# A hybrid decoder trunk on one core: the second layer's state chain in two stretches of four chunks in place of four of two

## What is computed

```python
r, k, v, z = rkvz[0], rkvz[1], rkvz[2], rkvz[3]      # xm[p] @ w[p], four projections
logw = -jax.nn.softplus(-(w0 + jnp.tanh(xm[4] @ w1) @ w2)) - 0.5
a = jax.nn.sigmoid(a0 + (xm[5] @ a1) @ a2)
...
def step(state, inp):
    rt, wt, kt, vt, kkt, at = inp
    sa = jnp.einsum("bhvk,bhk->bhv", state, -kkt)
    state = (state * wt[:, :, None, :] + sa[..., None] * (kkt * at)[:, :, None, :]
             + vt[..., None] * kt[:, :, None, :])
    return state, jnp.einsum("bhvk,bhk->bhv", state, rt)
...
out = (y * jax.nn.silu(z)) @ rw_w_out[j]
```

## Time and profile before

| what | value |
|---|---|
| median of three runs | 3538.35 us (3529.3 to 3553.95) |
| the profiled execution | 3545.52 us |
| its span in the profile | 3543.7 us |
| mean granted clock of TensorE | 0.971 |
| TensorE, matmuls | 3286.5 us busy, 93% |
| VectorE | 1604.9 us busy, 45% |
| ScalarE | 1314.0 us busy, 37% |
| GpSimd | 222.4 us busy, 6% |

### The profile page before, as it was taken

The page is one execution under the profiler, slowest core; times in us unless marked ns, Lnnn a source line. Parts: engine busy times, 40 slices in busy tenths (PEclk is TensorE's granted clock), DMA queues, the critical chain, the costliest instruction groups (busy, mean ns, idle before and its releaser), DMA issues.

```text
span 3543.7 us, 80467 instructions
## 1 busy us (share of the span) xinstructions
PE 3286.5 (93%) x35338; PEld 1989.4 (56%) x35338; DVE 1604.9 (45%) x3443; ACT 1314.0 (37%) x2492; POOL 222.4 (6%) x345
## 2 busy tenths in 40 slices
PE   2899999999999968999999999999999999999998
PEld 1555465556455535666566466556466656556663
DVE  7245254435534544344564244554244454244442
ACT  0343344343434353333453133444133453223332
POOL 0010001010001000000000000000000000000000
PEclk8999999999999988999999999999999989999999
DMA  8231322331224131112112212112212112121111
GB/s 333 73 97 49 120 84 85 96 97 48 82 86 121 49 108 38 39 39 63 38 39 68 79 39 63 26 51 63 78 39 67 33 39 62 46 77 39 39 61 42
DMA packets 275862, 247.53 MB, mean 70 GB/s; under 512 B 16253, under 2 KB 251961, under 8 KB 272953
## 3 DMA queue, kind: packets, MB, share of 16 engines
q1 hardware_dynamic: 273208, 233.99, 21.0%
q0 software_dynamic: 2304, 8.39, 0.7%
HBM read 217.17 MB, written 25.18 MB: 68 GB/s over the span
## 4 chain that ended last, share of the span: by engine, by line
PE 75%; DVE 12%; DMA 5%; ACT 5%; issue 2%; SPq 1%; DVEq 0%; ACTq 0%; another core or an unknown queue 0%
PE bank L679 20%; PE bank L539 14%; PE bank L648 7%; PE bank L765 4%; PE bank L778 4%; PE bank L536 3%; PE bank L774 3%; DVE xm L1561 3%; PE bank L568 2%; DVE arena L1622 2%; PE bank L690 2%; DMA xm<-in_ada_w 2%; PE bank L820 1%; DMA arena<-residual_scratch 1%; DVE arena L1632 1%
## 5 line engine op out<-in xcount | busy, mean ns | idle before, releaser
L679 PE MATMUL bank<-xm,wring 128*128 128x512 f32 x2048 | 933.6, 604 | 0.8 <-ACT arena L1104 0.8
L679 PEld LDWEIGHTS bank<-xm,wring 128*128 128x128 f32 x2048 | 383.2, 192 | 474.8 <-issue 462.4
L539 PE MATMUL bank<-arena,wring 128*128 128x512 f32 x1280 | 580.0, 593 | 12.5 <-ACT xm L969 5.1
L539 PEld LDWEIGHTS bank<-arena,wring 128*128 128x128 f32 x1280 | 231.0, 190 | 256.7 <-issue 246.0
L648 PE MATMUL bank<-wring,yT 128*128 128x512 f32 x776 | 340.2, 599 | 16.7 <-DVE yT L1681 5.4
L648 PEld LDWEIGHTS bank<-wring,yT 128*128 128x128 f32 x776 | 148.1, 192 | 204.9 <-issue 188.6
L1150 ACT COPY arena<-bank 128x256 f32<-128x256 f32 x256 | 96.4, 377 | 440.3 <-PE bank L778 440.3
L1837 POOL COPY r_Q<-ident 128x512 f32<-128x512 f32 x160 | 98.1, 613 | 2017.4 <-PE bank L778 2015.5
L1662 DVE COPY arena<-bank 128x64 f32<-128x64 f32 x256 | 57.3, 224 | 348.6 <-PE bank L810 342.8
L778 PE MATMUL bank<-arena,r_Q 64*64 64x32 f32 x5120 | 201.8, 222 | 0.2 <-issue 0.2
L765 PE MATMUL bank<-arena 64*64 64x32 f32 x5120 | 191.4, 221 | 1.6 <-DVE arena L1646 1.1
(11 more groups left out here) (278 smaller groups left out, 5097.2 us busy)
## 6 DMA issues: line engine op xcount, KB each, us to landing
wring<-in_rw_w_rkvz SPq DMA_DIRECT2D x128, 512.0 KB, 3.9
wring<-in_ev_w_in SPq DMA_DIRECT2D x96, 512.0 KB, 5.2
xm<-in_ada_w SPq DMA_DIRECT2D x16, 1536.0 KB, 12.0
wring<-in_ev_w_out SPq DMA_DIRECT2D x32, 512.0 KB, 5.3
wring<-in_rw_w_out SPq DMA_DIRECT2D x32, 512.0 KB, 5.5
layer_input<-arena SPq DMA_DIRECT2D x4, 2052.0 KB, 7.7
wring<-layer_input SPq DMA_DIRECT2D x16, 513.0 KB, 7.2
xm<-in_x POOLq DMA_DIRECT2D x16, 512.0 KB, 5.3
```

Source lines behind the costliest of these rows:

```text
L539: mm = pe.matmul(pj[:, :], w[:, k, :], hT[:, k, 1:1 + TB], start=(k == 0), stop=(k == KC - 1))
L679: mm = pe.matmul(bank[1 if m == PROJ_Z else 0][:, :], w[:, k, :], xmv[MIX_OF[m]][:, k, :], start=(k == 0), stop=(k == KC - 1))
```

## The change

Three lists of work change their order, one for each engine, and no instruction is added or removed. On TensorE quarter 0 comes behind projection K and the second gate matmul instead of in front of them, and quarter 2 comes behind projection Z instead of in front of it. The chunks of a unit then run as 0 to 3 and 4 to 7, with the key sum and projections R and Z in one run between them. ScalarE and VectorE have their parts moved likewise: gate, K's copy, the squares and both sigmoids in front of quarter 0; R's copy, decays, rates, finish and bonus in front of quarter 2. `INV_CUT`, the waits within the helpers, and SyncE's and GpSimd's programs stay as they are.

```diff
--- before.py
+++ after.py
@@ -876,20 +876,20 @@
                 if not inv:
                     pe.wait_ge(S["b0_free"], turn(BANK0, "v", v) + 1)
                     pe.wait_ge(S["b1_free"], turn(BANK1, "var", v - 1) + 1)
-                quarter(v, 0)
                 if pre:
                     lora_up(v + 2, 0)
                     project(v + 2, PROJ_K, 0, KC)
                     lora_up(v + 2, 1)
+                quarter(v, 0)
                 quarter(v, 1)
                 if pre:
                     key_sum(v + 2)
                     project(v + 2, PROJ_R, 0, KC)
-                quarter(v, 2)
                 if inv:
                     project(v + 1, PROJ_Z, 0, KC)
                 else:
                     pe.wait_ge(S["r_done"], 1 + v)
+                quarter(v, 2)
                 quarter(v, 3)
                 if (v + 3) % RP == 0 and v + 3 < NU:
                     lora_down((v + 3) // RP)
@@ -1186,7 +1186,6 @@
                     act.copy(r_yd, bank[1][:, :]).then_inc(S["b1_free"], 1)
                 if inv:
                     project_evac(v + 1, PROJ_V)
-                quarter_act(v, 0)
                 if pre:
                     lora_evac(v + 2, 0)
                 if v >= 0:
@@ -1199,6 +1198,7 @@
                     project_evac(v + 2, PROJ_K)
                     key_squares(v + 2)
                     lora_evac(v + 2, 1)
+                quarter_act(v, 0)
                 quarter_act(v, 1)
                 if pre:
                     act.wait_ge(S["r_tbm"], v + 3)
@@ -1213,7 +1213,6 @@
                     mix(B, MIX_W, 0, 5)
                 if second_:
                     mix(B, MIX_V, 0, 5)
-                quarter_act(v, 2)
                 if pre:
                     project_evac(v + 2, PROJ_R)
                     decays(v + 2)
@@ -1224,6 +1223,7 @@
                     mix(B, MIX_A)
                 if second_:
                     mix(B, MIX_V, 5, KC)
+                quarter_act(v, 2)
                 quarter_act(v, 3)
                 if inv:
                     project_evac(v + 1, PROJ_Z)
@@ -1701,7 +1701,6 @@
                     mix(B, MIX_K, 3, KC)
                 if inv:
                     rwkv_masks(v + 1)
-                rwkv_quarter(v, 0)
                 if v >= 0:
                     rwkv_gate(v)
                 if pre:
@@ -1710,6 +1709,7 @@
                     mix(B, MIX_R)
                 if third:
                     mix((v + 1) // RP, MIX_Z)
+                rwkv_quarter(v, 0)
                 rwkv_quarter(v, 1)
                 if pre:
                     rwkv_key(v + 2)
@@ -1717,7 +1717,6 @@
                     mix(B, MIX_W, 0, 5)
                 if second_:
                     mix(B, MIX_V, 0, 5)
-                rwkv_quarter(v, 2)
                 if pre:
                     rwkv_rates(v + 2)
                 if v >= 1:
@@ -1729,6 +1728,7 @@
                     mix(B, MIX_A)
                 if second_:
                     mix(B, MIX_V, 5, KC)
+                rwkv_quarter(v, 2)
                 rwkv_quarter(v, 3)
                 own.restart()
```

## The result

The changed kernel takes 3567.9 us, the median of 15 runs (3550.7 to 3580.8). The kernel before took 3553.95 in the 15 runs beside it (3529.3 to 3557.6). The ratio is 1.0052, with a 95% interval of 1.0035 to 1.0069 (the two medians lie 0.4% apart): slower by half a per cent, where the forecast, 3535 for 3538.35, was a ratio of 0.999. The profiled span went from 3543.7 to 3566.1 us and the mean granted clock from 0.971 to 0.961.

What follows compares the result with a forecast made beforehand. TensorE, busy for 93% of the span, was taken as the bound. Terms -0.8 (plain), +3, -2, 0, -1, +1 and -4 (clock) sum to -3.8 us: 3535 us from 3538.35; own range 3522 to 3550, stated range 3510 to 3575.

Steps and rivals of the forecast that it cites:

- Step 1: Plain period, chunk 0: the key run in front covers the masks' tail, gate and scan, so TensorE's wait goes, -0.49 us.
- Step 3: Plain period, chunk 1 to chunk 2: the joint loses its cover and line 810 waits for the new state, +0.34 us.
- step 4: Plain period, chunk 5 to chunk 6: line 810 likewise waits for VectorE's new state, +0.31 us.
- step 5: Plain period, R and Z joined in one run: one change of tile size in and one out are gone, -0.20 us.
- Steps 2, 6 and 7: Plain period: V's copy before K, other engines' work beside R and Z, and weight loads all stay hidden, no cost.
- v = 5, 13 and 21: Eleven mixes now before quarter 2: wait about 6.9 us against 5.3 and some 0.6; +1.0 each, +3 in all.
- v = 15: Periods with Z mixes: their wait of a microsecond moves from chunk 2 to chunk 0, net 0.
- The clock, -4: Of three half-clock falls behind chunk 0's idle time (v = 14, 22, 23), one was expected to go, -4 us.
- v = 14: Key run covers chunk 0's losses, but R's mixes leave 1.3 us idle there: net -0.7, three times, -2 us.
- Unit 30: Without K, 1.5 us of sigmoid idle time moves from chunk 2 to chunk 0; chunk 4 gets Z in front: -1 us.
- The falling clock: Rival, chance 0.14: clock falls in longer small-tile stretches, once per plain period +90 us, 3625 us; in both stretches 3715.
- The joints' rival: Rival, chance 0.12: exposed joints cost more, 1.3 us a plain period in all, giving 3561 us.

Runs made afterwards that it cites:

- e3: New order in the 21 plain periods only, old order in the others, against the kernel before: 3543.1 us, ratio 0.9976.
- e2: Only the second move (quarter 2 behind projection Z), quarter 0 left where it was, against the kernel before: 3566.7 us, ratio 1.0045.
- e7: Kernel before with idle VectorE additions put in front of chunk 2 in 13 plain periods: 3611.9 us, one run.
- e4: New order only in periods 5 to 7, 13 to 15, 21 to 23, 30 and 31, against the kernel before: 3575.4 us, ratio 1.0072.
- e1: Only the first move (quarter 0 behind the key run), quarter 2 left where it was, against the kernel before: 3545.4 us, ratio 0.9977.
- e13: Changed kernel, mixes whole, with an inverse part moved into the last gap of chunks 1 and 5: 3535.5 us, ratio 0.9946 to the kernel before.
- e6: Changed kernel with idle VectorE additions put in front of chunk 0 in 13 plain periods: 3678.3 us, one run.
- e8: Changed kernel with R and Z mixes split in halves and an inverse part in both joints' gaps: 3510.9 us, ratio 0.9899 to the kernel before.
- e10: First move only, R and Z mixes split, one inverse part in the last gap of chunk 1, against the kernel before: 3506.5 us, ratio 0.9883.
- e11: First move, split mixes and filled gap of chunk 1, but old order in v = 30 and 31, against the kernel before: 3503.9 us, ratio 0.987.

## Why the prediction was wrong

**The plain period** was right in kind and nearly so in size. Step 1 said -0.49 for chunk 0; it measured -0.75 (2.77 for 3.52 from line 810 to line 810), a little over the 0.7 that I had given as a bound and not taken. Step 3 said +0.34 and measured +0.34 (2.70 for 2.36), step 4 +0.31 and +0.30 (2.49 for 2.19), step 5 -0.20 and -0.19 (17.15 for 10.28 and 7.06). Steps 2, 6 and 7 cost nothing, as said: no plain period waits for line 1104 or in front of chunk 4. A period is 57.26 us for 57.54, so -0.28 where I had -0.04. Over 21 that is -6 at most and -4.6 by the trace; e3 confirms the sign. Nor does a row show the bounds of -13 and +15 behind the range of 3522 to 3550: the bounds worked out above it were -19, +13 and +26.

**v = 5, 13 and 21**: the wait in front of chunk 4 was to be 6.9 us and is 7.1. The three were to cost +3 and cost +6.0, since the half clock behind the wait now lasts over four chunks (17.1 us in v = 13 and 21, against 6.8 and 10.2). Busy time by stretch of the changed kernel, v = 13, chunks 4, 5 and 6, where full clock has 2.57, 2.49 and 2.57:

```profile
2286.06:2296.41 10.35, 3.28 (x93) 3.17 (x94) 8.89 (x16) 5.31 (x10) 0.00 (x0) 0.65 0.00 0
2296.41:2300.68 4.27, 4.15 (x90) 3.96 (x87) 1.30 (x5) 0.64 (x3) 0.61 (x1) 0.50 0.02 4
2300.68:2304.78 4.10, 4.10 (x95) 4.10 (x95) 0.73 (x3) 1.10 (x4) 0.38 (x1) 0.50 0.02 4
```

**v = 15** is the sentence that failed: "the Z mixes' wait of a microsecond moves from chunk 2 to chunk 0: 0". The wait did move, and grew to 1.33 and 1.68 us. But I priced its idle time alone, though the earlier trace rows showed what it is worth: idle time like it in front of chunks had cost 4.8 us by the clock. Behind 0.91 us at chunk 2 the clock fell in 4 of 12 such periods of the old order (the kernel before, e2, e3 and e7); behind 1.33 to 1.7 us at chunk 0 in 14 of 15 of the new, and each fall then lasts over three more chunks. That cost +20.4 us over the three periods in the profiled pair, nearly the whole of its 22.4; e4 has +19.3, e1, with one fall less, +10.8.

**The clock, -4**, failed with it. I took the falls for a stock that only shrinks: three there, one goes. I did not go through the new order and ask of each wait how many small-tile chunks follow it. Half clock rose by 77.9 us, and at the 8.7 us lost in the 20.5 of period 7 that is an estimate of 33 us, near the +31.9 that the mix periods and the end lost with their waits. v = 14 shows it too: I had put 1.3 us of idle time at its chunk 0 (by my own terms, 11.5 less 10.4, it is 1.1) and gave it no fall; the wait is 0.82 us, and the clock fell for 17.1 us behind it and for 3.4 at chunk 4. The period takes 69.0 us for the 65.9 of before, where I had -0.7.

**Unit 30** waits 2.25 us in front of chunk 0 where I had moved 1.5 there, and fell for 17.1 us: +2.3 where I had -1. Without the fall, in e4, it is -4.7.

**The start of the layer**, -7.3 us, was not in my sum at all. I counted from period 0. In period -1, before the change, TensorE waits 1.37 and 1.05 us for masks and runs two gate steps and K behind them in part at half clock. Timelines, first of the kernel before, then of the changed one:

```profile
1355.95 1.12 PE L765 MATMUL bank<-ident,arena 64*64 64x32 f32 x32 [1.37 <-DVE arena L1622]
1358.13 1.82 PE L765 MATMUL bank<-arena 64*64 64x32 f32 x32 [1.05 <-DVE arena L1646]
...
1365.30 8.72 PE L679 MATMUL bank<-xm,wring 128*128 128x512 f32 x16
```

```profile
1358.07 7.13 PE L679 MATMUL bank<-xm,wring 128*128 128x512 f32 x16
...
1366.18 1.12 PE L765 MATMUL bank<-ident,arena 64*64 64x32 f32 x32
```

With K in front, the masks are ready when line 765 comes, and K takes 7.13 us instead of 8.72. e1 and e3 have this gain (96.3 and 95.8 us up to period 0), e2 and e4 don't (102.7 and 102.9).

**The rivals.** The falling clock was the right mechanism in the wrong place. I had it as a property of long stretches, in all plain periods or none, and gave 0.14 for 3625 us. The runs show it as a property of idle time in front of a stretch. The Trainium skill's rule (TensorE: Matmul & The Clock Gate, section "A second HAM failure mode: psum-queue depth-cycling"), that moments of idle time between groups make the clock swing, did not hold for the 0.27 us of the joints: no plain period of e3 or of the changed kernel shows half clock by them. Nearer to it is the start of v = 6, 14 and 22 in the old order: three idle moments of 0.48, 0.62 and 0.84 us within 3.6 us brought a fall in 13 of 15 such periods, while the last of them alone, 0.82 us in the new order, did in 6 of 15. The joints' rival (3561 us) was near in time, but not by its own mechanism: it charged the joints in plain periods, which gained, and e13 shows that they cost where the clock has already fallen. As for size: in the two halves of the change, e3 gained 0.24% and e4 lost 0.72%, and my sum had -0.8 us for the first and -3 for the second.

What stays open is why the clock falls behind one wait and not behind another of the same length (2 of 13 in e6, v = 7 in e1, unit 30 in e1 and e4), how a filled joint shortens a fall, and why the two moves together cost more than the product of each.

## What to carry to other kernels

Price a wait by what runs behind it: in a kernel at full clock, a microsecond of idle time that made the clock fall cost another 3 to 5 us here in front of two chunks of small matmuls, and 7 to 8.5 in front of four, because the clock mostly came back in a run of full-size ones. So before work is regrouped into longer runs, go through every wait that will stand in front of one, in the rare periods first: eleven periods lost three times here what the other 21 gained (0.72% in e4 against 0.24% in e3). And once regrouped, take out what the old order left: work lumped on another engine can be halved to lie beside the large matmuls, and gaps that were covered by a moved step want a piece of filler work.

## What was unexpected of the hardware

- A fall outlasts its cause by far. TensorE was busy for 4.32 of 4.46 and 4.75 of 4.75 us in chunks 1 and 2 of period 7, and stayed at 0.50; the clock came back beside 128x512 matmuls. In e8 and e13 it came back among small tiles too, where no idle time lay between the chunks; the 0.14 us in chunk 1 above are the visible difference.
- Falls by the length of the wait of line 820 at chunk 0, in the five runs with the mixes whole and the new order there (the changed kernel, e1, e4, e6, e13): none in plain periods by the joints' 0.27 us; at 0.82 us (v = 6, 14, 22) 6 of 15; at 1.05 us 11 of 13; at 1.33 to 1.7 us (v = 7, 15, 23) 14 of 15. Length isn't all: at 2.25 us unit 30 fell in three of these five, and several short moments close together, as above, did more than one.
- The same instructions at half clock: a chunk of 2.70 us takes 4.46 (1.65 times), one of 2.82 takes 4.75 (1.68 times), so by this estimate about a third of a chunk of small tiles doesn't go by the clock.
- Runs of one kernel spread over 30 us (3550.7 to 3580.8 for the changed one), about three falls' worth. e10 and e8, with fewer waits to fall behind, spread over 3.5 and 6.7 us, though in 5 and 4 runs only, and e11 over 11.4 in 6.
